# Four rows to one sum, four column groups to one conditioning unit: a decoder step with expert retrieval on one core

## The reference, cut to what matters

```python
mod = jax.nn.silu(c) @ w_ada[l] + b_ada[l]              # 9 conditioning rows, 6 x 1024 columns
sh1, sc1, g1, sh2, sc2, g2 = jnp.split(mod, 6, axis=-1)
h = modulate(rmsnorm(x, norm1[l]), sh1, sc1)
mix, pb, cb, lh = mixer_block(h, ...)                   # projections, conv, RG-LRU scan, pooling, gates, output
x = x + g1[:, None, :] * mix
h = modulate(rmsnorm(x, norm2[l]), sh2, sc2)
x = x + g2[:, None, :] * peer_block(h, w_q[l], sub_keys[l], expert_u[l], expert_v[l])
y = rmsnorm(x, final_norm)
# peer_block, for a token: 8 heads choose 16 of 128*128 experts each, so 128 experts
act = jax.nn.gelu(jnp.einsum('nd,nhkd->nhk', xb, expert_u[idx]))
wts = softmax(best_s) * act
return jnp.einsum('nhk,nhkd->nd', wts, expert_v[idx])
```

## Time and profile before

| | us |
|---|---|
| median of 3 runs | 2075.16 (2071.17 to 2078.55) |
| the profiled execution | 2075.3 |
| its span on the core | 2073.5 |
| TensorE busy | 1761.0 (85%) |
| VectorE busy | 1321.4 (64%) |
| ACT busy | 1074.8 (52%) |
| POOL busy | 761.9 (37%) |
| moved by DMA | 730.12 MB, mean 352 GB/s |

### The profile page before, as it was taken

The page is one execution under the profiler, slowest core; times in us unless marked ns, Lnnn a source line. Parts: engine busy times, 40 slices in busy tenths (PEclk is TensorE's granted clock), DMA queues, the critical chain, the costliest instruction groups (busy, mean ns, idle before and its releaser), DMA issues.

```text
span 2073.5 us, 17144 instructions
## 1 busy us (share of the span) xinstructions
PE 1761.0 (85%) x5376; PEld 907.2 (44%) x5376; DVE 1321.4 (64%) x2952; ACT 1074.8 (52%) x2080; POOL 761.9 (37%) x582
## 2 busy tenths in 40 slices
PE   7999985799888999997998777777778778777776
PEld 3599983344344555553553232232322223332222
DVE  1452247888988867756755666667666667666544
ACT  1162024433476442344445666667666667666665
POOL 0000003333323334343324445544555444554663
PEclk9999997899989999998999999999999999999999
DMA  8755649799969999997979999999999999999996
GB/s 279 263 205 198 207 169 398 292 355 385 373 250 351 338 377 386 357 371 289 355 275 372 402 393 416 412 411 398 411 413 415 405 421 401 407 415 416 404 422 281
DMA packets 104659, 730.12 MB, mean 352 GB/s; under 512 B 12956, under 2 KB 13350, under 8 KB 16879
## 3 DMA queue, kind: packets, MB, share of 16 engines
q0 software_dynamic: 82976, 604.02, 73.1%
q1 hardware_dynamic: 20196, 122.34, 16.3%
q10 hardware_dynamic: 1396, 2.67, 0.4%
HBM read 725.92 MB, written 3.06 MB: 352 GB/s over the span
## 4 chain that ended last, share of the span: by engine, by line
PE 49%; DMA 25%; DVE 14%; ACT 8%; issue 3%; POOL 1%; SPq 0%; DVEq 0%; ACTq 0%; POOLq 0%
PE bank L600 25%; DMA t_uv_rows<-in_expert_uv,t_arena 22%; PE v_sum L684 6%; DVE t_uv_rows L1272 6%; PE v_sum L685 6%; PE bank L556 4%; ACT t_uv_rows L855 4%; PE v_sum L679 3%; PE v_sum L680 3%; DMA t_uv_rows<-in_expert_uv,t_idx 2%; DVE t_uv_rows L1280 1%; ACT t_wts L849 1%; PE bank L625 1%; PE bank L577 1%; ACT L847 1%
## 5 line engine op out<-in xcount | busy, mean ns | idle before, releaser
L1272 DVE CUSTOM_DVE_ANT_0 t_uv_rows<-t_uv_rows,t_arena 128x1024 f32<-128x1024 f32 x384 | 468.8, 1225 | 353.4 <-DMA t_uv_rows<-in_expert_uv,t_arena 348.7
L514 POOL DMA_INDIRECT t_uv_rows<-in_expert_uv,t_arena x384 | 500.5, 1303 | 519.7 <-PE v_sum L680 320.8
L600 PE MATMUL bank<-t_arena,t_weights 128*128 128x192 f32 (+1 forms) x2560 | 647.7, 411 | 10.6 <-issue 9.7
L855 ACT ACTIVATE t_uv_rows<-t_uv_rows,t_wts 128x1024 f32<-128x1024 f32 x480 | 551.2, 1148 | 15.6
L600 PEld LDWEIGHTS bank<-t_arena,t_weights 128*128 128x128 f32 x2560 | 454.6, 192 | 214.4 <-issue 67.1
L514 POOL DMA_INDIRECT t_uv_rows<-in_expert_uv,t_idx x192 | 260.2, 1355 | 766.5 <-DVEq L1257 307.0
L847 ACT ACTIVATE t_gelus<-t_dots 128x1 f32<-128x1 f32 x576 | 114.2, 198 | 584.5 <-DVE t_dots L1272 583.7
L684 PE MATMUL v_sum<-t_uv_rows,t_ident 128*128 128x512 f32 (+1 forms) x576 | 318.4, 635 | 115.3 <-DVE t_uv_rows L1280 62.4
L679 PE MATMUL v_sum<-t_uv_rows,t_ident 128*128 128x512 f32 x384 | 220.5, 657 | 161.1 <-ACT t_uv_rows L855 161.1
L685 PE MATMUL v_sum<-t_uv_rows,t_ident 128*128 128x512 f32 (+1 forms) x576 | 302.9, 608 | 0.0
L1272 DVE CUSTOM_DVE_ANT_0 t_uv_rows<-t_uv_rows,t_tok 128x1024 f32<-128x1024 f32 x192 | 230.2, 1220 | 67.6 <-DMA t_uv_rows<-in_expert_uv,t_idx 67.3
(11 more groups left out here) (194 smaller groups left out, 1024.7 us busy)
## 6 DMA issues: line engine op xcount, KB each, us to landing
t_weights<-in_w_in SPq DMA_DIRECT2D x40, 1024.0 KB, 5.2
t_weights<-in_w_ada SPq DMA_DIRECT2D x24, 1024.0 KB, 4.9
t_weights<-in_w_q SPq DMA_DIRECT2D x16, 1024.0 KB, 7.1
t_weights<-in_w_branch_a SPq DMA_DIRECT2D x8, 1024.0 KB, 7.7
t_weights<-in_w_branch_b SPq DMA_DIRECT2D x8, 1024.0 KB, 6.9
t_weights<-in_w_out SPq DMA_DIRECT2D x8, 1024.0 KB, 5.5
t_uv_rows<-in_expert_uv,t_arena POOLq DMA_INDIRECT x384, 9.6
t_weights<-in_keys_t SPq DMA_DIRECT2D x20, 256.0 KB, 6.4
```

What stands on the lines that cost most here:

```text
L514: pool.indirect_dma_start(out=row(r), out_offset=None, in_=A["expert_uv"], in_offset=bass.IndirectOffsetOnAxis(ap=idx_of(t)[:, n:n + 1], a ...
L600: ins = nc.tensor.matmul(bank[:, 0:n], w[:, k, j * P:(j + 1) * P], src[:, k, :], start=k == 0, stop=k == KT - 1)
L855: nc.scalar.activation(v, v, ACT.Copy, scale=wts[:, col(r)]).then_inc(scaled_done, 1)
L1272: V.tensor_tensor_reduce(out=u, in0=u, in1=h2_rows(t), scale=1.0, scalar=0.0, op0=ALU.mult, op1=ALU.add, accum_out=dots[:, col(r)]).then_i ...
```

## The change

Three things change, and the planner's places with them.

- *Rows.* Each pair has a mode. "lone" (pairs 0 to 8, every third pair from 26 to 47, and all from 96): both rows scaled on ACT, both added by TensorE. "pair" (as `merged` before): all others but pairs 48 to 87. There, "open" and "close" alternate: ACT scales the first row of four, VectorE adds the second, third and fourth on (`add_on`, three adds), and TensorE adds the fourth alone. A fetch waits for the add or the sum that frees its slot (`ADDED`, `SUMMED`).
- *Conditioning.* `silu_c` is padded from 9 to 32 columns with zeros. The eight matmuls of a unit go to four column groups (`tile_position` 0, 32, 64, 96), two to each group, so each group holds a quarter of the sum on its own 32 partitions. VectorE adds bank and bias rows on all 128 partitions, and the turn becomes a matmul with `fold`, which adds the four quarters (the later `select` matmuls likewise). The bias comes by four small transfers on POOL's queue, each behind a clear of its rows, in place of two broadcast loads on SP. Units 0 to 7 come first, 8 and 9 around the norm, and 10 to 23 one after each third unit of group 0's mixer, with the second turn after unit 19.
- *Norm and places.* `scale` and `shift` are cut into halves of four feature blocks each. The norm of group 1 starts one pair earlier (5, 6, 7, 7, 8), `RATE` of VectorE is 3.5 for 3.2, the choice of tile 1's second quarter moves two pairs or so earlier, and the last eight queries of group 1 go to pairs 96, 99, ... 117.

```diff
+LONE_BEFORE, LONE_AMONG, FOURS = 9, range(26, 48, 3), (48, 88)
+def mode(p):
+    if p < LONE_BEFORE or p >= PAIR0[2] or p in LONE_AMONG:
+        return "lone"
+    if FOURS[0] <= p < FOURS[1]:
+        return ("open", "close")[(p - FOURS[0]) % 2]
+    return "pair"
...
-    return [(kind, g, which) for kind in ("norm", "scale", "shift")]
+    return [(kind, g, which) for kind in ("norm", "scale0", "scale1", "shift0", "shift1")]
...
-RATE, DEBT, SAVED = (5.6, 3.2, 4.6), (1.0, 3.0, 5.0), (5.6, 4.0, 4.6)
+RATE, DEBT, SAVED = (5.6, 3.5, 4.6), (1.0, 3.0, 5.0), (5.6, 4.0, 4.6)
...
-    norm, scale, shift = norm_units(0, 0)
-    start = [[("ada", 0, i)] for i in range(8)] + [[("modT", 0, 0)], [("ada", 0, 8), ("square", 0, 0)], [norm], [("ada", 0, 9)], [scale], [shift]]
-    start += [[("ada", 0, i)] for i in range(10, 20)] + [[("modT", 0, 1)]] + [[u] for u in mixer_units(0)]
-    start += [[("ada", 0, 20)], [("ada", 0, 21)], [("tok", 0, 0)]]
+    norm, *scale = norm_units(0, 0)
+    start = [[("ada", 0, i)] for i in range(8)] + [[("modT", 0, 0), ("square", 0, 0)], [norm], [("ada", 0, 8)], [scale[0]], [("ada", 0, 9)]] + [[u] for u in scale[1:]]
+    later = [("ada", 0, i) for i in range(10, 24)]
+    for n, unit in enumerate(mixer_units(0)):
+        start.append([unit])
+        if n % 3 == 2 and later:
+            start.append([later.pop(0)])
+            if later and later[0][2] == 20:
+                start.append([("modT", 0, 1)])
+    start += [[("tok", 0, 0)]]
...
-    pack(queries[4:], places, ready + 1)
+    pack(queries[4:8], places, ready + 1)
+    for n, unit in enumerate(queries[8:]):
+        places[PAIR0[2] + 3 * n].append(unit)
...
+            nc.gpsimd.memset(silu_c[:, :, NR:], 0.0).then_inc(ones_done, 1)
             nc.gpsimd.memset(ones[:, :], 1.0).then_inc(ones_done, 1)
+            for n, (first, last) in enumerate(((0, 8), (8, 14), (14, 20), (20, 24))):
+                rows = mod_rows(first, last - first)
+                nc.gpsimd.memset(rows, 0.0).then_inc(mod_zeroed, 1)
+                pool.wait_ge(mod_zeroed, n + 1)
+                pool.dma_start(rows[NR:NR + 1, :], A["b_ada"][:, first * WB:last * WB]).then_inc(bias_in, 16)
...
-                    old = (r - NROW) // 2
-                    if r % 2:
-                        pool.wait_ge(summed, old + 1)
-                    elif merged(old):
-                        pool.wait_ge(paired_done, merged_count(old))
+                    old = r - NROW
+                    if old in ADDED:
+                        pool.wait_ge(added, ADDED[old])
                     else:
-                        pool.wait_ge(first_summed, split_count(old))
+                        pool.wait_ge(summed, SUMMED[old])
...
-                for k in range(KT):
-                    ins = nc.tensor.matmul(bank[0:NR, 0:WB], silu_c[:, k, :], w[:, k, :], start=k == 0, stop=k == KT - 1)
+                for half in range(2):
+                    for q in range(4):
+                        k = 2 * q + half
+                        ins = nc.tensor.matmul(bank[32 * q:32 * q + 32, 0:WB], silu_c[:, k, :], w[:, k, :], start=half == 0, stop=half == 1,
+                                               tile_position=(0, 32 * q))
...
-                    ins = nc.tensor.transpose(bank[:, (j - first) * NR:(j - first + 1) * NR], mod_rows[:, j * P:(j + 1) * P], ident[0:NR, 0:NR])
+                    rows = mod_rows(j // 2)[:, j % 2 * P:(j % 2 + 1) * P]
+                    ins = nc.tensor.matmul(bank[:, (j - first) * NR:(j - first + 1) * NR], rows, fold[:, :], start=True, stop=True)
...
-            def combine(p):
-                one, two = row(2 * p)[:, D:], row(2 * p + 1)[:, D:]
-                dve.wait_ge(scaled_done, scaled_count(2 * p))
-                dve.wait_ge(weight_done, 2 * p + 2)
-                V.scalar_tensor_tensor(out=two, in0=two, scalar=wts[:, col(2 * p + 1)], in1=one, op0=ALU.mult, op1=ALU.add).then_inc(paired_done, 1)
+            def add_on(r):
+                if r - 1 in ADDED:
+                    dve.wait_ge(added, ADDED[r - 1])
+                else:
+                    dve.wait_ge(scaled_done, SCALED[r])
+                dve.wait_ge(weight_done, r + 2)
+                v = row(r + 1)[:, D:]
+                V.scalar_tensor_tensor(out=v, in0=v, scalar=wts[:, col(r + 1)], in1=row(r)[:, D:], op0=ALU.mult, op1=ALU.add).then_inc(added, 1)
...
-                    if merged(PAIR0[g] + b):
-                        combine(PAIR0[g] + b)
+                    p = PAIR0[g] + b
+                    if mode(p) == "close":
+                        add_on(2 * p - 1)
+                    if mode(p) != "lone":
+                        add_on(2 * p)
```

More of the change, by code:

```diff
@@ L40, with row_counts @@
 PAIR0 = tuple(8 * n for n in STEP0)
-def merged(p):
-    return p < PAIR0[2]
-def merged_count(p):
-    return sum(merged(q) for q in range(p + 1))
-def split_count(p):
-    return p + 1 - merged_count(p)
-def scaled_count(r):
-    p = r // 2
-    before = sum(1 if merged(q) else 2 for q in range(p))
-    return before + (r % 2 + 1 if not merged(p) else 1)
+LONE_BEFORE, LONE_AMONG, FOURS = 9, range(26, 48, 3), (48, 88)
[5 more added lines that the diff above has]
+    return "pair"
+def row_counts():
+    scaled, added, summed = {}, {}, {}
+    for p in range(PAIR0[-1] + PAIRS_OF[-1]):
+        way, one, two = mode(p), 2 * p, 2 * p + 1
+        if way != "close":
+            scaled[one] = len(scaled) + 1
+        if way == "lone":
+            scaled[two] = len(scaled) + 1
+            summed[one] = len(summed) + 1
+        if way == "close":
+            added[one - 1] = len(added) + 1
+        if way != "lone":
+            added[one] = len(added) + 1
+        if way != "open":
+            summed[two] = len(summed) + 1
+    return scaled, added, summed
+SCALED, ADDED, SUMMED = row_counts()
 VEC = ("norm1", "norm2", "pool_scale", "conv_b", "b_rg", "b_ig", "lru_lambda",
@@ L743, in norm, with shift @@
                 nc.scalar.activation(rstd[:, 0:n], ms[:, 0:n], ACT.Sqrt).then_inc(std_done, 1)
-            def shift(g, which):
+            def shift(g, which, half):
                 s, p, n = sizes(g)
@@ L748, in shift @@
                 act.wait_ge(coef_done, 2 + which)
-                act.wait_ge(h_scaled, 2 * g + which + 1)
-                for k in range(KT):
+                act.wait_ge(h_scaled, 2 * (2 * g + which) + half + 1)
+                for k in range(4 * half, 4 * half + 4):
                     nc.scalar.activation(h[:, k, s:n], h[:, k, s:n], ACT.Identity, scale=coef[:, which, k, SB:NR],
@@ L1001, in norm, with scale @@
                 dve.sem_inc(ms_done, 1)
-            def scale(g, which):
+            def scale(g, which, half):
                 s, p, n = sizes(g)
@@ L1013, in scale @@
                     dve.wait_ge(ready["q"], nth(("q", 0, 15)))
[L1014 removed]
+                four = slice(4 * half, 4 * half + 4)
+                mark(V.tensor_tensor(h[:, four, :], x[:, four, :], r, ALU.mult), h_scaled, 2 * m + half + 1)
+                if half == 0:
+                    return
                 if s:
```

131 lines of the change are left out of this document (67 added, 64 removed).

## The result

The changed kernel took 2061.8 us (median; the kernel before, beside it, 2074.7). The ratio is 0.9941, with a 95% interval from 0.9926 to 0.9956: 13 us faster where 59 were forecast, and outside the range. Its profiled execution has a span of 2060.0 us.

The account below looks back on a forecast made before the run. Binding engines were taken to vary by stage, often TensorE, with DMA full at the end. Gains of 4.5 + 10 + 5 + 13 + 15 + 11, about 59 us, took 2075.3 to 2016 us; range 1990 to 2048.

Parts of the forecast that it names:

- The start: Conditioning and trunk up to the first row fetch: rows start 4 to 5 us earlier; bounds 13 earlier, 23 later.
- not its sum: Pairs 26 to 47: the higher VectorE rate packs units two or three pairs tighter, moving work without changing its total.
- Unit: Conditioning unit in four column groups: 1.75 us taken, between 0.9 (four at once) and 3.5 (no overlap; rival, chance 0.2).
- Turns: Conditioning's turns: the second, in the first group's trunk, was priced at 1.7 us.
- Waits and clock: First group's trunk: new weight waits of 1 to 4 us, some 13 in all (18 at 0.9 us a unit).
- S2: Stage of the first group's trunk, after conditioning: 57.2 us of TensorE work before, forecast to take 96 us.
- The bound "13 earlier": Start of the rows if a conditioning unit takes 0.9 us: 13 us earlier.
- Pairs 0 to 8: Rows added one at a time early: the stage of pairs 0 to 9 falls from 100 to 90 us, gaining 10.
- Singles among 26 to 47: Eight single pairs there relieve VectorE but load TensorE to 156.7 us: gain 5 us, at most 9.
- Fours: Pairs 48 to 79: one TensorE sum fewer per two pairs; 231 to 218 us, gain 13, bounds 0 and 24.
- The rivals about the fours: Pairs 48 on: fours change nothing, 2029 us, chance 0.15; or starve the fetches, say 2085 us, chance 0.06.
- Queries and second norm: Pairs 80 to 109: spread queries gain 15 us to pair 95 and 15 after, with 4 given back at the end.

Follow-up runs that it names:

- experiment 16: Changed kernel with only the planner's numbers of before put back (VectorE rate 3.2, laid units at 38, 40, 42, 43): 2053.4 us, ratio 0.9895.
- the base: Changed kernel with the conditioning of the kernel before (one column group, 20 units ahead of the trunk, transposes, bias by SP): 2046.3 us, ratio 0.9887.
- experiment 3: Changed kernel with all matmuls of both turns issued twice (extra work): 2084.3 us in one execution.
- experiment 4: Changed kernel with idle matmuls filling TensorE's waits for weight blocks in conditioning and first trunk (extra work): 2055.9 us in one execution.
- experiment 7: The base with the single pairs 0 to 8 added in twos again: 2056.1 us, ratio 0.9923.
- experiment 9: The base with the planner's numbers of before (VectorE rate 3.2, laid units at 38, 40, 42, 43): 2031.0 us, ratio 0.9806.
- experiment 5: The base without fours, pairs 48 to 87 added in twos again: 2056.7 us, ratio 0.9939.
- experiment 13: Kernel of experiment 9 with the norm in one piece and the second tile's first query at pair 84: 2038.6 us, ratio 0.9813.
- experiment 2: Changed kernel with column groups kept but conditioning units 10 to 19 ahead of the trunk again: 2048.4 us, ratio 0.9882.

## Why the prediction was wrong, step by step

Two steps failed above all. The start was priced without the clock and with the wrong turn, and came 25 us off. And the denser plan, which was to move work and "not its sum", was priced at nothing and costs 8 us in the change (experiment 16) and 15 in the base.

**The start** (forecast 4.5 earlier, came 20.3 later) failed in three terms, and not in the unit, the one that I took for uncertain.

- *Unit.* 1.75 was too high; 1.07 is near the bound of 0.9. The Trainium skill, TensorEngine Tiling (Array Packing), Key Properties, has tiles working in parallel, and the trace agrees (1.07 against 3.54). By the Trainium skill, TensorE: Matmul & The Clock Gate, Part 3, the loads of column groups, which share their rows, would not overlap running matmuls; here they did: sixteen loads of 0.11 us, 1.7 us one after another, fit into the 1.07.
- *Turns.* I gave the second turn, by matmuls with `fold`, the price of transposes with nine rows (1.7 for 1.61 before), and the first none of its own. They load 128x128 weights, twice per matmul. The rate stood in the earlier trace rows: 127.95 us for 673 loads, 0.19 each, so 32 and 48 of them are 6.1 and 9.1 us. Measured 6.97 and 8.17, 12.4 us more than the transposes took, and experiment 3 shows that nearly all of it is paid.
- *Waits and clock.* By my way through the order a faster unit makes longer waits (18 us at 0.9); at 1.07 they came to 16.9 where I summed 13. That the engine runs slower behind each wait I did not price in S2 at all. Of the 110.4 us, 57.2 are trunk, 15.0 the fourteen units, 8.2 the turn, 16.9 the waits and 0.6 the wait for the turn. The 12.5 left over are nearly all the clock: in its timeline the rows behind waits take 11.4 us longer in all than the same rows at full clock, and experiment 4 took 6 from this stretch and 10 from the whole start. The bound "13 earlier" for the fast unit had the turn at 1.7 and the clock at nothing, so it was no bound: the fast unit came nearly true and the start was 20 later. Its own terms, with 18 of waits (57.2 + 14 x 0.9 + 1.7 + 18 = 89.5), give 11 and not 13.
- *Units 20 and 21.* They "gave nothing where they stood", by the prediction. Without them TensorE idles through the second norm of group 0 and then works more slowly. The same sixteen records in the changed kernel:

```profile
295.05 3.65 PE L679 MATMUL bank<-t_ident,t_arena 128*128 128x128 f32 x16 [6.61 <-ACT t_arena L781]
```

and in the kernel before:

```profile
277.08 1.94 PE L649 MATMUL bank<-t_ident,t_arena 128*128 128x128 f32 x16 [0.40 <-issue]
```

From the fourth `u` unit to the first fetch it took 3.6 us longer, where 1 less was forecast; the halves gave their 1 there (9.4 us from the squares to these records, 10.2 before).

The bias rows cost nothing, as forecast: POOL's last clear ended at 9.24 us, and VectorE began only at 17.09, behind the load of `iota`.

**Pairs 0 to 8** (10): right in size; 10 by experiment 7, 7 of them by pair 9. The table shows only 4 at pair 10, and 4 more by pair 27, in a stage where I had nothing: without the early singles the base takes 4 us longer than the kernel before from first fetch to pair 9 (85.9 against 81.9), by something else in the change that was not found.

**Singles among 26 to 47** (5): right beside the plan of before (6.5, with overlapping intervals), wrong beside the plan of the change (-4.8). The step that failed is "which moves work, not its sum". The sum did not change, but the work moved out of pairs where the DMA is near full (share 0.97) into pairs where it is not (0.86) and TensorE is the busiest engine (127.10 of 136.10); I had worked out 156.7 of TensorE work for that stage and not asked what the plan adds to it. 15 us by experiment 9, 8 by experiment 16.

**Fours** (13, plus their part past pair 80): 10 by experiment 5, TensorE no longer full (209.39 of 226.00), the DMA at 377 GB/s in this stage. Mechanism and bounds held. In the table above they are hidden, since the stage pays for the plan first: from pair 48 to 52 alone the changed kernel lost 12.7 us. So a pair took 7.06 us (226.0 / 32) with POOL waiting for VectorE's add, which I had written down as a sign of being wrong; the sign misled, for from pair 52 to 79 it took 6.70, against 7.20 before. The rivals about the fours both fell: nothing by experiment 5, and starving, which needed a landing of 15 us or so, by the rows, which landed 9.5 us after their issue (median). Mixed traffic, which had not done better than 369 GB/s in a long stage before, did 389 in pairs 52 to 79.

**Queries and second norm** (30, with 4 given back): 33 and 6 came. The sum was right, which was partly luck, for its split was not: the queries' place is worth 14, and 13 to 16 belong to the halves and to the query that they move behind a sum. I had put the halves at 1 us and read TensorE's hole as the loss; the hole stayed as long, and about half of the loss or more was which instruction stood first behind it (experiment 13).

The parts don't add up: taken out of the base one at a time, the four that gain make 47.2 us, and plan and singles together lose 8.8 (2046.3 to 2037.5), where the base gains 26. The queries, the norm and the fours may earn on the same rows in store; that is not shown, and how they share the gain was not resolved.

## What to carry to other kernels

Before you shorten work that waits for transfers, ask what the engine does in the time won: here it waited, and then ran the next units slower. When a plan "only moves" work, compare the slack of both places with the other edits in. And at a stall, look not only at its length but at what stands first in the engine's order behind it: a sum that frees buffers belongs ahead of a unit that must wait.

## What the runs showed of the hardware

Eight fp32 matmuls of 128x32 by 128x256 in four column groups take 1.07 us where eight of 128x9 without groups take 3.54: 3.3 times as fast, at full clock. The same sixteen records also took 1.93 us, in stretches where TensorE waited for each block (in experiment 2 busy 28.74 of 50 us, mean granted clock 0.69, between the levels of 1.2 and 2.4 GHz), and idle matmuls in its waits made one execution of the changed kernel 6 us faster. Row fetches beside weight blocks reached 389 GB/s in pairs 52 to 79 and 394 in pairs 96 to 109 (410 there in experiment 9, with two blocks among them), against 369 at most in a long stage before and 410 without weights.
